# Softmax normalisation of the latent-attention heads issued on VectorE in place of GpSimd

## What is computed

```python
for j in range(s // Q_BLOCK):                 # 4 blocks of 128 queries
    q0, q1 = j * Q_BLOCK, (j + 1) * Q_BLOCK
    kend = q1                                 # block j sees (j+1)*128 keys
    logits = (jnp.einsum('bqhd,bkhd->bhqk', q_nope[:, q0:q1], k_nope[:, :kend])
              + jnp.einsum('bqhr,bkr->bhqk', q_rope[:, q0:q1], k_rope[:, :kend]))
    logits = logits.astype(jnp.float32) * scale
    mask = (pos[None, :kend] // CHUNK) <= (pos[q0:q1, None] // CHUNK)
    logits = jnp.where(mask[None, None], logits, NEG_INF)
    p = jax.nn.softmax(logits, axis=-1).astype(v.dtype)
    outs.append(jnp.einsum('bhqk,bkhd->bqhd', p, v[:, :kend]))
```

## Time and profile before

| | |
|---|---|
| median of 3 runs | 1103.98 (1101.59, 1103.98, 1104.29) |
| the profiled execution | 1101.59, its span 1099.7 |
| granted TensorE clock, mean | 0.996 |
| busy | PE 98%, DVE 75%, ACT 43%, POOL 20% |
| the attention's heads | about 606 to 700 of the span |

### The profile page before, as it was taken

How to read it: one execution, slowest core, us unless ns; L and a number is a source line. 1 busy time by engine, 2 the same in 40 slices (tenths; PEclk the granted TensorE clock), 3 DMA queues, 4 the chain that set the end, 5 groups by cost and what they waited for, 6 DMA issues and landing times.

```text
span 1099.7 us, 18513 instructions
## 1 busy us (share of the span) xinstructions
PE 1073.4 (98%) x6630; PEld 949.4 (86%) x6630; DVE 830.1 (75%) x1118; ACT 470.4 (43%) x692; POOL 222.7 (20%) x209
## 2 busy tenths in 40 slices
PE   8999999899999999999999999988999999999997
PEld 7888888899999998888877766777999999978887
DVE  5865659999999999344578677399999999984443
ACT  6212236444444446222346477264444454552122
POOL 6000001322332320111200244013323322201010
PEclk9999999999999999999999999999999999999999
DMA  7333332233233323333322101022333233333321
GB/s 197 100 93 110 97 95 77 77 115 104 87 114 114 99 89 111 106 105 103 110 72 73 28 27 52 1 77 78 115 114 98 93 114 114 95 106 88 105 65 77
DMA packets 144038, 101.66 MB, mean 92 GB/s; under 512 B 3912, under 2 KB 142336, under 8 KB 144000
## 3 DMA queue, kind: packets, MB, share of 16 engines
q1 hardware_dynamic: 143648, 100.61, 30.4%
q0 software_dynamic: 320, 0.55, 0.2%
q10 hardware_dynamic: 32, 0.01, 0.0%
HBM read 99.06 MB, written 2.10 MB: 92 GB/s over the span
## 4 chain that ended last, share of the span: by engine, by line
PE 85%; DVE 8%; ACT 3%; issue 2%; DMA 1%; SPq 0%; DVEq 0%; ACTq 0%
PE ps L374 26%; PE ps L376 26%; PE ps L375 26%; PE ps L1596 3%; PE ps L1657 2%; PE ps L1673 2%; DVE wgt_lo L358 1%; DVE inv L448 1%; DVE op_w_lo L519 1%; ACT hid_hi L753 1%; DMA x_nat<-in_x 1%; DVE x_op_lo L1052 1%; DVE inv_lat L448 1%; ACT op_w_hi L513 1%; ACT x_op_hi L717 0%
## 5 line engine op out<-in xcount | busy, mean ns | idle before, releaser
L374 PE MATMUL ps<-x_op_hi,op_w_hi 128*128 128x256 f32 x1232 | 350.1, 284 | 10.1 <-DVE op_w_lo L519 6.8
L375 PE MATMUL ps<-x_op_lo,op_w_hi 128*128 128x256 f32 x1232 | 349.3, 284 | 0.0
L376 PE MATMUL ps<-x_op_hi,op_w_lo 128*128 128x256 f32 x1232 | 349.3, 284 | 0.0
L374 PEld LDWEIGHTS ps<-x_op_hi,op_w_hi 128*128 128x128 f32 x1232 | 237.1, 192 | 12.7 <-DVE op_w_lo L519 7.1
L375 PEld LDWEIGHTS ps<-x_op_lo,op_w_hi 128*128 128x128 f32 x1232 | 237.2, 193 | 0.1
L376 PEld LDWEIGHTS ps<-x_op_hi,op_w_lo 128*128 128x128 f32 x1232 | 237.2, 193 | 0.0
L374 PE MATMUL ps<-hid_hi,wgt_hi 128*128 128x512 f32 (+1 forms) x550 | 211.8, 385 | 2.1 <-DVE hid_lo L1109 2.1
L376 PE MATMUL ps<-hid_hi,wgt_lo 128*128 128x512 f32 (+1 forms) x550 | 209.5, 381 | 0.0
L375 PE MATMUL ps<-hid_lo,wgt_hi 128*128 128x512 f32 (+1 forms) x550 | 209.5, 381 | 0.0
L358 DVE TENSOR_TENSOR wgt_lo<-raw,wgt_hi 128x1024 fp32r<-128x1024 f32 (+4 forms) x131 | 137.8, 1069 | 88.4 <-ACT wgt_hi L349 87.1
L349 ACT ACTIVATE wgt_hi<-raw 128x1024 fp32r<-128x1024 f32 (+4 forms) x131 | 107.0, 831 | 147.1 <-PE ps L376 145.3
(11 more groups left out here) (166 smaller groups left out, 1234.2 us busy)
## 6 DMA issues: line engine op xcount, KB each, us to landing
pair_raw<-in_ffn_w_gate SPq DMA_DIRECT2D x22, 1024.0 KB, 5.4
pair_raw<-in_ffn_w_up SPq DMA_DIRECT2D x22, 1024.0 KB, 5.3
raw<-in_conv_w_in SPq DMA_DIRECT2D x24, 512.0 KB, 3.8
raw<-in_ffn_w_down SPq DMA_DIRECT2D x32, 384.0 KB, 3.4
raw<-in_ffn_w_down SPq DMA_DIRECT2D x32, 320.0 KB, 3.0
raw<-in_conv_w_out SPq DMA_DIRECT2D x8, 512.0 KB, 3.8
raw<-in_mla_w_o SPq DMA_DIRECT2D x8, 512.0 KB, 3.8
x_nat<-in_x SPq DMA_DIRECT2D x4, 512.0 KB, 7.0
```

Source lines behind the costliest of these rows:

```text
L374: nc.tensor.matmul(acc, wh, xh, start=first, stop=False)
L375: nc.tensor.matmul(acc, wh, xl, start=False, stop=False)
L376: return nc.tensor.matmul(acc, wl, xh, start=False, stop=last)
```

## The change

POOL no longer normalises. The multiplications of `prob` by the row's factor stand in DVE's stream, each pair of them directly behind its reciprocal, with a wait for that reciprocal (`rec_done`) between. `factors(hd)` and the old `normalise(hd)` become one function `normalise(hd)` on DVE, at each of the places where `factors(hd)` stood. The operation goes from a multiplication by the factor and by 1.0 to a single multiplication by the factor. The wait of DVE for `p_ready` goes, since DVE itself now raises it.

```diff
--- before.py
+++ after.py
@@ -635,20 +635,7 @@
             clear_sum(0)
             for m in range(X_POOL):
                 add_square(0, m, x_copied, m + 1)
-            def normalise(hd):
-
-                par = hd % 2
-                for n, js in enumerate(((3, 1), (2, 0))):
-                    pool.wait_ge(rec_done, 2 * hd + n + 1)
-                    for j in js:
-                        blk = prob[:, par, L_OFF[j]:L_OFF[j] + (j + 1) * P]
-                        ins = nc.gpsimd.tensor_scalar(blk, blk, rec[:, par, j:j + 1], 1.0, ALU.mult, ALU.mult)
-                ins.then_inc(p_ready, 1)
-
             for n, name in ((1, "conv_out"), (2, "down0"), (3, "mla_out"), (4, "down1")):
-                if n == 3:
-                    for hd in range(HEADS):
-                        normalise(hd)
                 if n % 2:
                     weight_sums(n // 2, 0, 0)
                     ffn(n // 2)
@@ -1304,15 +1291,18 @@
                     if n != 2:
                         ins.then_inc(s_read, 1)
 
-            def factors(hd):
+            def normalise(hd):
 
                 par = hd % 2
                 for n, js in enumerate(((3, 1), (2, 0))):
                     ve.wait_ge(exp_done, 2 * hd + n + 1)
-                    if hd >= 2:
-                        ve.wait_ge(p_ready, hd - 1)
                     two = slice(js[1], js[0] + 1, 2)
                     nc.vector.reciprocal(rec[:, par, two], sums[:, par, two]).then_inc(rec_done, 1)
+                    ve.wait_ge(rec_done, 2 * hd + n + 1)
+                    for j in js:
+                        blk = prob[:, par, L_OFF[j]:L_OFF[j] + (j + 1) * P]
+                        ins = nc.vector.tensor_scalar(blk, blk, rec[:, par, j:j + 1], None, ALU.mult)
+                ins.then_inc(p_ready, 1)
 
             def back_copies(hd):
 
@@ -1338,11 +1328,11 @@
             row_low(0)
             rotate(8)
             rotate(9)
-            factors(0)
+            normalise(0)
             rotate(10)
             row_low(1)
             rotate(11)
-            factors(1)
+            normalise(1)
             back_copies(0)
             rotate(12)
             rotate(13)
@@ -1351,13 +1341,13 @@
                 if i == 1:
                     rotate(14)
                 back_copies(2 * i - 1)
-                factors(2 * i)
+                normalise(2 * i)
                 if i == 1:
                     rotate(15)
                 row_low(2 * i + 1)
                 if 3 <= i < 7:
                     unit_lo(ve, "mla_out", 0, i - 3)
-                factors(2 * i + 1)
+                normalise(2 * i + 1)
                 head_out(i - 1)
                 back_copies(2 * i)
             back_copies(HEADS - 1)
```

## The result

| | before | after |
|---|---|---|
| median | 1103.41 (4 runs, 1101.59 to 1104.29) | 1108.77 (4 runs, 1107.82 to 1109.96) |
| ratio | | 1.0051, 95% interval 1.0039 to 1.0063 |
| profiled execution | 1101.59, span 1099.7 | 1107.82, span 1105.9 |

What follows compares the result with a forecast made beforehand. DVE's chain was taken to set the period in pairs that split a weight, with PE at its edge. Terms 0.52 + 0.92 + 4 × 1.20 = 6.24 gave 1110.2 on the median, forecast as 1110.0, range 1106.5 to 1114.5.

Steps and rivals of the forecast that it cites:

- What bounds the kernel: In pairs that split a weight, DVE's chain sets the period of 9.41; PE waits 0.26 before the odd head's turn.
- The cost of a pass: On DVE 0.29, 0.35, 0.42 and 0.49 for 128, 256, 384 and 512 columns; a head takes 1.65, a pair 3.30.
- The price by the Trainium skill: Rival for DVE's passes: 58 cycles plus columns over speed-up, fixed cost 0.06 not 0.22; 1107.4 on the median, chance 0.03.
- A pair with a weight: Pairs 3 to 6 in the heads: DVE's period goes from 9.41 to 10.61, +1.20 for each pair.
- A pair without one: Pair 2 in the heads, without a weight: DVE's period becomes 10.34 in place of 9.42, +0.92.
- The start and the end: Heads 0 to 3: +0.52, pair 2 starting at 632.79; pair 7: no loss, turn(15) due at 696.77.
- What is taken away: POOL's 64 passes in the heads, 33 in all; nothing waited for them, so removing them gives back nothing.
- The sum: Over the heads, 0.52 + 0.92 + 4 × 1.20 = 6.24; 1110.2 on the median, forecast as 1110.0.
- The slow pass: Rival: DVE's passes run at the speed of a two-input operation; +10.5, so 1114.5 on the median, chance 0.10.
- Absorption: Rival: DVE's idle time of 1.93 per pair takes up all the passes; 1104, chance 0.08.
- DVE's other steps shorten: Rival: with POOL silent, DVE's other steps in the heads get quicker; about 1103 even then, chance 0.04.
- The clock: Rival: PE's wait of 1.46 per pair lowers its clock to 1.2 GHz; one pair there gives 1117.9, chance 0.04.

Runs made afterwards that it cites:

- e_even_part0: Against the kernel before, only part 0 of the even heads' passes moved to DVE, the other 48 left on POOL: ratio 1.0005, the heads 0.03 less.
- e_swap_before: The kernel before (POOL normalises) with back_copies(2i) ahead of head_out(i-1) in DVE's stream: ratio 0.9993, the heads 1.57 less.
- e_none: Against the kernel before, all 64 normalising passes left out, turn waiting for the reciprocals, output not the reference's: ratio 1.0000, the heads 83.71.
- e_double: The changed kernel with every pass issued twice on DVE, first into an unread scratch buffer: median 1124.36, ratio 1.0193 to the kernel before.
- e_swap_again: Second measurement of the kernel before with back_copies(2i) ahead of head_out(i-1): ratio 0.9986, median 1102.15 against 1103.46, the heads 1.56 less.

## Why the prediction was right, step by step

- **What bounds the kernel.** Right: in the heads the chain on DVE, with its waits for ACT, sets the period, and PE waits for it at one place. e_even_part0 shows that DVE's work as such costs nothing, and e_swap_before that the same work in another order, without the wait of 0.32, has a shorter period.
- **The cost of a pass.** Right in duration. In spacing it was 0.03 to 0.04 too dear per part: reciprocal and two passes take 0.86 and 0.72 (611.49 to 612.35 and to 613.07, head 0 after) where 0.89 and 0.76 stood. From the reciprocal to the first pass it is 0.19 in place of 0.21, and the overlap of a pass with the step behind it is nearer 0.09 than 0.08. DVE's busy time was to rise by 25 and rose by 19.7: the 25 adds up durations, in which the overlaps count twice. The price by the Trainium skill ("VectorE: DVE Perf Modes", the section on the TRN2 errata; an estimate of 0.33 for 512 columns) is not what any run shows; 0.487 is. The prediction sets that estimate beside a duration and then adds it up as a spacing (0.7 a pair, 3.5 in all). With the overlap of 0.08 taken off, as for the rows, the same chain gives an estimate of 0.3 a pair and 1.6 in all. The spacing behind 512 columns is 0.40 (0.75 for two passes, less the 0.348 of the second).
- **A pair with a weight.** The period was forecast as 10.61 and is 10.50; the row of the odd head 4.63, and is 4.61. The waits left were forecast as 0.41, 0 and 0; they are 0.36, 0 and 0. PE's gap was forecast as 1.5 at the turns 7 to 13, and is 1.35 or 1.36; the 0.77 at turn(5) was not forecast.
- **A pair without one.** 10.34 was forecast, 10.27 came: the changed kernel's `row_low` starts at 632.71 in pair 2 and at 642.98 in pair 3.
- **The start and the end.** Pair 2 was to begin at 632.79, or 0.52 late; it begins at 632.71, of which 0.05 is the head start's own shift, so 0.38 late. At turn(15) no wait was forecast and none is there. It was due at 696.77 and came at 696.18.
- **What is taken away.** Nothing was expected from POOL's 33, and e_none shows nothing.
- **The sum.** 6.24 was forecast for the heads, and 5.60 is measured; the 0.64 are the small spacing errors (4 × 0.11 + 0.07 + 0.14). That the profiled executions differ by just the 6.2 of the forecast is chance: 0.6 of it lies outside the heads, told of below.
- **The rivals.** The slow pass: out by the rows. Absorption: true for 16 of the 64 passes, those of e_even_part0, and for the first part of the others' cost. Its condition was also too lenient, since it added up DVE's steps alone: by the prediction's own layout `head_out` can't come less than 3.88 after the odd head's `row_low`, so part 1 of the even head would have had to fit in the 0.12 of the reciprocal that stood there. DVE's other steps shorten: out by e_none. The clock: not in the heads of the changed kernel, whose gaps are 1.35 at a granted clock of 1.00; seen in e_double behind gaps from 2.35 on. The support that the prediction took from the earlier trace rows was luck: in seven of the eleven traces the clock falls behind that very gap (last section).

One reading of the prediction was off, without harm to the sum. PE's slack in a pair of the kernel before was taken to be the 0.26 of the bracket, so PE's own work to be 9.15. In e_swap_before and e_swap_again, where PE never waits, the same turns come every 8.95. The real slack was 0.45 or 0.46 in each of three pairs, and 0.18 in the one before them, where the trace shows no gap at all. The changed kernel agrees: 10.50 less 8.95 is 1.55, and the gap reads 1.36. The ends of matmuls are modelled, so an idle gap of PE reads 0.19 too short here; distances of starts don't. That is also why 1.6 was to be had by the swap where the rival in the prediction allowed 0.8, three times 0.26.

## What to carry to other kernels

Price a step that moves to another engine on that engine's timeline, not by its busy share: 16 passes in the right place cost nothing, 32 cost 2.2 or 3.2 by their place, 64 cost 5.6, and 128 cost 21. Taking work off an engine that nobody waits for gives nothing back, however idle or slow it looks. Where an engine's chain sets the pace, look for a short wait in the middle of it and let a step that is ready go first: swapping two lines won 1.6 in the heads here, and no placement of the passes won anything.

## What the runs showed of the hardware that was not expected

- **The clock and short gaps.** In the earlier trace rows a gap of PE of 2.33 left the granted clock at 1.00. All eleven traces have that gap, of 2.32 to 2.36, and in seven of them the granted clock of 590 to 600 is 0.83. Here it is in e_swap_before:

```profile
593.08 0.50 PE L1638 MATMUL ps<-wgt_hi,hid_hi 128*128 128x512 f32 x1 [2.34 <-DVE v_nat L1213]
...
590.00:600.00 10.00, 7.66 (x27) 5.84 (x26) 7.16 (x11) 6.84 (x13) 0.00 (x0) 0.83 0.00 1
```

The same holds for PE's first long gap behind the heads. The kernel before has it at 737.71, e_swap_before at 737.72. Each gap is shown with the busy times behind it, first of the kernel before, then of e_swap_before:

```profile
737.71 0.39 PE L374 MATMUL ps<-x_op_hi,op_w_hi 128*128 128x256 f32 x1 [2.84 <-DVE x_op_lo L1052]
...
737.00:743.00 6.00, 5.29 (x41) 4.97 (x41) 5.44 (x10) 4.80 (x8) 0.25 (x1) 1.00 0.01 3
```

```profile
737.72 0.58 PE L374 MATMUL ps<-x_op_hi,op_w_hi 128*128 128x256 f32 x1 [2.83 <-DVE x_op_lo L1052]
...
737.00:743.00 6.00, 5.28 (x24) 5.29 (x25) 5.45 (x10) 4.80 (x8) 0.25 (x1) 0.50 0.01 3
```

One stays at the 2.4 GHz level and the other runs at 1.2 GHz, behind equal gaps. In e_double a gap of 2.35 was followed by slow transposes (1.98 for ten) and one of 1.86 was not. The gaps of 1.35 in the changed kernel recur in four pairs and never lower the clock, so the warning of the Trainium skill ("TensorE: Matmul & The Clock Gate", the section on HAM oscillation) on recurring gaps does not bear on gaps as short as these. From 2.3 to 2.8 it goes either way, and no run here says what decides. One trace is thus not enough to call such a gap harmless.

- **Where the runs scatter.** The heads repeat to within 0.03 in kernels that should be equal there (83.74, 83.71, 83.71; 82.17, 82.18, 82.18). Much of what differs elsewhere goes with the clock behind those two gaps. From the end of the first gap to `row_low(0)` it is 13.7 to 13.8 in the four traces with 1.00 from 590 to 600, and 15.3 to 15.4 in the seven with 0.83. From turn(15) to the span's end it is 409.2 in the kernel before and 409.0 in e_none, whose granted clock stays at 1.00 in the first groups of the feed-forward part (the 20 that begin 40 after turn(15)). In the nine others it is 0.83 or 0.91 there, and 409.7 to 411.0 to the end. The changed kernel has 409.7, and e_even_part0, which costs nothing in the heads, has 411.0. So the 0.5 between the two profiled executions lies within this scatter and can't be put down to the change; the 5.6 of the measured ratio agrees with the heads alone.
